# Side gate of an encoder layer: bias added by one-row products on TensorE, sigmoid read from the banks by ScalarE

## The reference

```python
    f = moe(x.reshape(B * T, D), ...).reshape(B, T, D)
    x = layer_norm(ALPHA * x + f, ln2_g, ln2_b)
    return x + jax.nn.sigmoid(x @ w_ple_gate + b_ple_gate) * (p_l @ w_ple_proj)
```

## Time and profile before

| | |
|---|---|
| median of 3 runs | 1488.61 us (1481.96 to 1497.39) |
| profiled execution | 1481.6 us, of which the span of instructions is 1479.8 us |
| PE busy | 1404.2 us, 95% of the span |
| DVE busy | 601.0 us, 41% |
| ACT busy | 275.6 us, 19% |
| gate products (L1442), both layers | 117.2 us of PE, 256 instructions |

### The profile page before, as it was taken

How to read it: one execution, slowest core, us unless ns; L and a number is a source line. 1 busy time by engine, 2 the same in 40 slices (tenths; PEclk the granted TensorE clock), 3 DMA queues, 4 the chain that set the end, 5 groups by cost and what they waited for, 6 DMA issues and landing times.

```text
span 1479.8 us, 20569 instructions
## 1 busy us (share of the span) xinstructions
PE 1404.2 (95%) x6970; PEld 727.9 (49%) x6970; DVE 601.0 (41%) x1224; ACT 275.6 (19%) x671; POOL 117.9 (8%) x137
## 2 busy tenths in 40 slices
PE   7999999898899999998999999989989999999898
PEld 3787446453344443443457874464533444433344
DVE  5086785545210110106530867855453110101356
ACT  1211335212100110011131013442121001000112
POOL 2100000110000000004000000011100000000300
PEclk9999999999999999999999999999999999999999
DMA  8714003354399999948031240033544999999821
GB/s 299 261 59 151 25 1 118 143 193 153 132 414 426 427 427 425 393 178 291 0 130 58 78 153 3 1 118 143 194 152 136 380 428 426 427 427 426 323 69 47
DMA packets 80940, 319.47 MB, mean 216 GB/s; under 512 B 12684, under 2 KB 15044, under 8 KB 56300
## 3 DMA queue, kind: packets, MB, share of 16 engines
q1 hardware_dynamic: 66772, 272.19, 47.0%
q0 software_dynamic: 9280, 29.68, 5.4%
q10 hardware_dynamic: 4824, 16.75, 2.8%
HBM read 429.21 MB, written 29.67 MB: 310 GB/s over the span
## 4 chain that ended last, share of the span: by engine, by line
PE 79%; DMA 7%; DVE 5%; issue 3%; SPq 2%; ACT 2%; DVEq 1%; POOL 0%; ACTq 0%; POOLq 0%
PE psum L1362 17%; PE psum L953 12%; PE psum L1389 9%; PE psum L1442 8%; PE psum L1021 8%; PE psum L1225 7%; PE psum L923 4%; DMA region<-in_w_exp_up_dram 3%; PE psum L892 2%; PE psum L871 1%; PE psum L1363 1%; PE psum L1276 1%; PE psum L1341 1%; PE psum L1006 1%; SPq L709 1%
## 5 line engine op out<-in xcount | busy, mean ns | idle before, releaser
L1362 PE MATMUL psum<-ring,xT 128*64 128x512 f32 x800 | 355.6, 596 | 9.1 <-DMA region<-in_w_exp_gate_dram 4.0
L1363 PE MATMUL psum<-region,xT 128*64 128x512 f32 x800 | 356.5, 597 | 0.0
L1362 PEld LDWEIGHTS psum<-ring,xT 128*64 128x64 f32 x800 | 107.2, 138 | 210.9 <-issue 210.8
L1389 PE MATMUL psum<-ring,region 128*64 128x512 f32 x400 | 176.2, 592 | 4.4 <-issue 2.8
L953 PE MATMUL psum<-xT,ring 128*128 128x272 f32 x768 | 176.5, 393 | 0.0
L1390 PE MATMUL psum<-region 128*64 128x512 f32 x400 | 176.3, 593 | 0.0
L953 PEld LDWEIGHTS psum<-xT,ring 128*128 128x128 f32 x768 | 145.8, 190 | 30.1
L2233 DVE COPY region<-psum 128x512 f32<-128x512 f32 x23 | 15.9, 691 | 319.7 <-PE psum L1390 319.7
L1021 PE MATMUL psum<-ring,xT 128*128 128x512 f32 (+1 forms) x288 | 132.5, 603 | 0.6 <-DVE region L1882 0.6
L1442 PE MATMUL psum<-ring,xT 128*128 128x512 f32 x256 | 117.2, 614 | 1.7 <-DMA ring<-in_w_ple_gate_dram 0.9
L778 POOL TENSOR_TENSOR rr<-rq,half 128x1 f32<-128x1 f32 (+4 forms) x41 | 56.9, 1387 | 716.6 <-DVE rq L1748 267.7
(11 more groups left out here) (286 smaller groups left out, 1456.9 us busy)
## 6 DMA issues: line engine op xcount, KB each, us to landing
region<-in_w_exp_gate_dram SPq DMA_DIRECT2D x54, 1024.0 KB
ring<-in_w_exp_gate_dram SPq DMA_DIRECT2D x54, 1024.0 KB
region<-in_w_exp_up_dram SPq DMA_DIRECT2D x54, 1024.0 KB
ring<-in_w_exp_up_dram SPq DMA_DIRECT2D x54, 1024.0 KB
ring<-in_w_exp_down_dram SPq DMA_DIRECT2D x54, 1024.0 KB
region<-in_w_exp_down_dram SPq DMA_DIRECT2D x54, 1024.0 KB
ring<-in_w_in_dram SPq DMA_DIRECT2D x24, 1024.0 KB, 8.4
expert_results<-region ACTq DMA_DIRECT2D x23, 512.0 KB, 7.7
```

The costliest lines, as they stand in the source:

```text
L1362: pe.matmul(bank[b][front, :], xeT[:, kc, front], ring[:, BLOCK_SLOT[u], kc % 4, :], start=kc == 0, stop=kc == KC - 1)
L1363: m = pe.matmul(bank[b][last, :], xeT[:, kc, last], back[:, UNIT_ROOM[u], kc % 4, :], start=kc == 0, stop=kc == KC - 1)
L1389: pe.matmul(bank[5 + half][front, :], hT[:, 2 * n + q, front], ring[:, BLOCK_SLOT[u], 2 * q + half, :], start=n + q == 0, stop=n + q == 2)
```

## The change

Four things are changed in the side-gate stage, in both layers.

- PE begins each half of tiles 0 to 3 with one product of a row of ones (`ones[0:1, :]`, set once at the start) by the bias row `bple[0:1, :]`, 128 x 512 out of a contraction of one row. The eight products that follow add to it. For tile 4 it is four such products of 32 x 128 a half. PE also waits, once a layer, for `hw_zero` and for `ln2p_in`.
- ACT takes the sigmoid straight out of the bank into `gt` (tile 4: in four quarters into `ye`) and frees the bank. For tiles 1 to 3 it first waits for `x_ready` of the tile before, whose `gt` DVE must have read. `gates(t - 2)` now stands ahead of the turned tile t.
- DVE loses the two sums of each tile, and the sums of tile 4.
- The semaphore `pg_sum` and the copies `sample_out("pg", n)` go.

```diff
@@ PE
                 turn_tile(l, "x2", x2_ready, 0)
+                pe.wait_ge(hw_zero, 1)
+                pe.wait_ge(ln2p_in, 48 * (l + 1))
                 for t in range(TILES):
                     turned(l, ("x2", t, 0))
                     turned(l, ("x2", t, 1))
...
                         if t == 4:
-                            m = sample_sum(pe, B(key), range(KC), ...)
+                            pe.sem_inc(pe_pass, 1)
+                            for c in range(4):
+                                pe.matmul(B(key)[DEC * c:DEC * c + DEC, 0:P], ones[0:1, 0:DEC], bple[0:1, n * 512 + c * P:n * 512 + (c + 1) * P], start=True, stop=False)
+                            m = sample_sum(pe, B(key), range(KC), ..., begun=True)
                             m.then_inc(full[use(key)], 1)
                             continue
+                        pe.matmul(B(key)[0:ROWS[t], :], ones[0:1, 0:ROWS[t]], bple[0:1, n * 512:(n + 1) * 512], start=True, stop=False)
                         for kc in range(KC):
...
-                            m = pe.matmul(B(key)[0:ROWS[t], :], xT[:, kc, span(t)], slot(u)[:, kc % 4, :], start=kc == 0, stop=kc == KC - 1)
+                            m = pe.matmul(B(key)[0:ROWS[t], :], xT[:, kc, span(t)], slot(u)[:, kc % 4, :], start=False, stop=kc == KC - 1)
@@ ACT
         def gates(sc, l, t):
+            if 0 < t < 4:
+                sc.wait_ge(x_ready, TILES * (l + 1) + t)
             for n in range(2):
-                sc.wait_ge(pg_sum, 2 * (TILES * l + t) + n + 1)
-                sc.activation(gt[0:ROWS[t], n * 512:(n + 1) * 512], gt[0:ROWS[t], n * 512:(n + 1) * 512], ACT.Sigmoid).then_inc(pg_sig, 1)
+                key = ("pg", t, n)
+                c = slice(n * 512, (n + 1) * 512)
+                sc.wait_ge(full[use(key)], taken(l, key) + 1)
+                if t == 4:
+                    m = quarters(sc, ye[0:DEC, c], B(key), ACT.Sigmoid)
+                else:
+                    m = sc.activation(gt[:, c], B(key)[:, :], ACT.Sigmoid)
+                m.then_inc(free[use(key)], 1)
+                sc.drain()
+                sc.sem_inc(pg_sig, 1)
...
                 for t in range(TILES):
+                    if t > 1:
+                        gates(sc, l, t - 2)
                     for s in range(2):
...
-                    if t > 1:
-                        gates(sc, l, t - 2)
                 gates(sc, l, TILES - 2)
                 if l + 1 < DEPTH:
                     x0_turned(l + 1, 0)
-                for n in range(2):
-                    sample_out("pg", n)
                 gates(sc, l, TILES - 1)
@@ DVE
                 def gate_add(t):
...
-                    for n in range(2):
-                        key = ("pg", t, n)
-                        c = slice(n * 512, (n + 1) * 512)
-                        if t == 4:
-                            ve.wait_ge(sample_ready, 4 * l + 2 + n + 1)
-                            ve.tensor_tensor(gt[0:r, c], ye[0:r, c], bple[0:r, c], ALU.add)
-                        else:
-                            filled(l, key)
-                            ve.tensor_tensor(gt[0:r, c], B(key)[0:r, :], bple[0:r, c], ALU.add)
-                        ve.drain()
-                        ve.sem_inc(pg_sum, 1)
-                        if t < 4:
-                            ve.sem_inc(free[use(key)], 1)
                     for n in range(2):
                         c = slice(n * 512, (n + 1) * 512)
                         ve.wait_ge(pg_sig, 2 * (TILES * l + t) + n + 1)
```

More of the change, by code:

```diff
@@ L492, in encoder_step @@
         sample_ready = sem("sample_product_ready")
-        pg_sum = sem("ple_gate_sum")
         pg_sig = sem("ple_gate_sig")
@@ L862, in rows_out, with sample_sum @@
             m.then_inc(oT_full, 1)
-        def sample_sum(pe, out, chunks, rows, weights):
+        def sample_sum(pe, out, chunks, rows, weights, begun=False):
             pe.sem_inc(pe_pass, 1)
@@ L870, in sample_sum @@
                 for c in range(4):
-                    m = pe.matmul(out[DEC * c:DEC * c + DEC, 0:P], rows(kc), weights(kc)[:, c * P:(c + 1) * P], start=kc == 0, stop=kc == KC - 1)
+                    m = pe.matmul(out[DEC * c:DEC * c + DEC, 0:P], rows(kc), weights(kc)[:, c * P:(c + 1) * P], start=kc == 0 and not begun, stop=kc == KC - 1)
             return m
@@ L1434, in _ @@
                         if t == 4:
-                            m = sample_sum(pe, B(key), range(KC), lambda kc: xT[:, kc, SEQ:TOK], lambda kc: slot(("pg", n, kc // 4))[:, kc % 4, :])
+                            pe.sem_inc(pe_pass, 1)
+                            for c in range(4):
+                                pe.matmul(B(key)[DEC * c:DEC * c + DEC, 0:P], ones[0:1, 0:DEC], bple[0:1, n * 512 + c * P:n * 512 + (c + 1) * P], start=True, stop=False)
+                            m = sample_sum(pe, B(key), range(KC), lambda kc: xT[:, kc, SEQ:TOK], lambda kc: slot(("pg", n, kc // 4))[:, kc % 4, :], begun=True)
                             m.then_inc(full[use(key)], 1)
                             continue
+                        pe.matmul(B(key)[0:ROWS[t], :], ones[0:1, 0:ROWS[t]], bple[0:1, n * 512:(n + 1) * 512], start=True, stop=False)
                         for kc in range(KC):
@@ L1463, in values, with quarters @@
             sc.activation(o_tok[:, i % 2, :], bank[6 + i % 2][:, :], ACT.Copy).then_inc(sq_done, 1)
-        def quarters(sc, dst, src):
+        def quarters(sc, dst, src, func=ACT.Copy):
             for c in range(4):
-                m = sc.activation(dst[:, c * P:(c + 1) * P], src[DEC * c:DEC * c + DEC, 0:P], ACT.Copy)
+                m = sc.activation(dst[:, c * P:(c + 1) * P], src[DEC * c:DEC * c + DEC, 0:P], func)
             return m
         def gates(sc, l, t):
+            if 0 < t < 4:
+                sc.wait_ge(x_ready, TILES * (l + 1) + t)
             for n in range(2):
-                sc.wait_ge(pg_sum, 2 * (TILES * l + t) + n + 1)
-                sc.activation(gt[0:ROWS[t], n * 512:(n + 1) * 512], gt[0:ROWS[t], n * 512:(n + 1) * 512], ACT.Sigmoid).then_inc(pg_sig, 1)
+                key = ("pg", t, n)
[8 more added lines that the diff above has]
+                sc.sem_inc(pg_sig, 1)
         @block.scalar
@@ L2049, in _ @@
                         if t == 4:
-                            ve.wait_ge(sample_ready, 4 * l + n + 1)
+                            ve.wait_ge(sample_ready, 2 * l + n + 1)
                             ve.scalar_tensor_tensor(xs, xs, ALPHA, ye[0:r, n * 512:(n + 1) * 512], ALU.mult, ALU.add)
@@ L2277, in gate_add @@
                 def gate_add(t):
-                    r = ROWS[t]
+                    r, gate = ROWS[t], ye if t == 4 else gt
                     ve.drain()
-                    for n in range(2):
-                        key = ("pg", t, n)
-                        c = slice(n * 512, (n + 1) * 512)
-                        if t == 4:
-                            ve.wait_ge(sample_ready, 4 * l + 2 + n + 1)
-                            ve.tensor_tensor(gt[0:r, c], ye[0:r, c], bple[0:r, c], ALU.add)
-                        else:
-                            filled(l, key)
-                            ve.tensor_tensor(gt[0:r, c], B(key)[0:r, :], bple[0:r, c], ALU.add)
-                        ve.drain()
-                        ve.sem_inc(pg_sum, 1)
-                        if t < 4:
-                            ve.sem_inc(free[use(key)], 1)
                     for n in range(2):
@@ L2295, in gate_add @@
                         ve.wait_ge(pg_sig, 2 * (TILES * l + t) + n + 1)
-                        ve.tensor_tensor(gt[0:r, c], gt[0:r, c], plp[0:r, PLP_AT[t], c], ALU.mult)
+                        ve.tensor_tensor(gate[0:r, c], gate[0:r, c], plp[0:r, PLP_AT[t], c], ALU.mult)
                     ve.drain()
-                    ve.tensor_tensor(x[0:r, t, :], x[0:r, t, :], gt[0:r, :], ALU.add).then_inc(x_ready, 1)
+                    ve.tensor_tensor(x[0:r, t, :], x[0:r, t, :], gate[0:r, :], ALU.add).then_inc(x_ready, 1)
                 ve.wait_ge(ln2p_in, 48 * (l + 1))
```

## The result

| | before | after |
|---|---|---|
| median | 1488.86 us (1481.96 to 1497.39, 4 runs) | 1512.19 us (1505.41 to 1513.65, 4 runs) |
| profiled execution | 1481.6 us, span 1479.8 | 1511.1 us, span 1509.2 |
| mean granted clock of it | 0.988 | 0.979 |

The ratio of after to before is 1.0152, with an interval of 1.0114 to 1.0191: the change makes the kernel some 23 us slower. The page of after shows DVE's share down and PE's busy time up; of that only a part is the new products.

The account below looks back on a forecast made before the run. PE's instructions were taken to bound the side-gate stage. Added products 20.0 us, less 0.15 hidden and 1.43 at the end, gave 18.4 us: 1507.0 us on the median of 1488.61, range 1495 to 1516.

Parts of the forecast that it names:

- PE's instructions are the path in this stage: Side-gate stage: PE sets the time; what is taken from DVE is worth nothing except in the last 4.57 us.
- The columns, 0.86 us a product: Tiles 0 to 3: each one-row product is two float32 instructions of 512 columns at 0.43 us each.
- The shape, 0.28 us: Each one-row product between full-shaped ones: going to another array shape and back costs 0.28 us, bounds 0 and 0.40.
- The sample tile, 0.9 us a layer: Tile 4: eight added instructions of 128 columns a half, 0.45 us a half with the way back.
- What hides it: 0.15 us in layer 1: Layer 1's stage start: waiting for the gate's weights covers 0.15 us of added PE work; layer 0's waits hide none.
- The end, 1.43 us less: Chain over ACT and DVE behind PE's last product: 3.14 us against 4.57.
- What is moved costs nothing: Moved gates, sigmoids and bank releases on ACT: covered by some 8 us of slack, so costed at nothing.
- that rival: PE's turn of tile 3 waits on DVE's 11.2 us stall; change frees up to 22.4 us: 1484.6 us, chance 3%.
- The clock's stretch at the stage's start: Rival: one-row product lengthens the half-rate clock stretch at both stage starts by 1.6 us each: 1510.2 us, chance 10%.
- The only-columns rival: Change of shape costs nothing for one-row products: 13.1 us slower, 1501.7 us on the median, chance 13%.

Follow-up runs that it names:

- run without products: Changed kernel with the row-of-ones products taken out and the gate's bias left out: median 1484.2 us, ratio 0.997 to the kernel before.
- 128-row run: Changed kernel with bias products contracting 128 rows of 1/128 instead of one row of ones: median 1499.6 us, ratio 1.0104 to the kernel before.

## Why the prediction was right

The time lies in the range that was given, and the sign and the bound of 1% were forecast; the sum was 18.4 us, 19.9 are measured at equal clock, 23 between the medians of the first runs. The median of after lies 5 us above the number that was given; it is in the range because the range's upper end was taken from the slowest run of before. Point by point:

- *PE's instructions are the path in this stage.* Right. Products alone cost what the whole change costs (+20.8 against 19.9 and 1.4 of gain), and the rest of the change leaves PE's timeline as it was.
- *The columns, 0.86 us a product.* Right to the hundredth: 8.60 - 7.74 between full-shaped neighbours.
- *The shape, 0.28 us.* This term was too small. It is 0.39 where both neighbours are full-shaped, so the row of the gathered sums (0.40) was the nearer one, and not that of the short contraction, which I took. By sixteen products the difference would be 1.8 us; where a neighbour has another shape already (the gathered sums and the transposes of the sample tile), one product costs 0.93 to 0.99 us, so some of it comes back. The rule of the Trainium skill (TensorEngine Tiling (Array Packing), Key Properties) that a change of tiling mode drains TensorE agrees with the trace here: the surcharge is there with one row and gone with 128.
- *The sample tile, 0.9 us a layer.* 771.80 - 767.33 = 4.47 us against 3.63 before: 0.84. Right.
- *What hides it: 0.15 us in layer 1.* Not seen: the first product starts 0.89 us behind the turned tile's transposes, like the first product before, and there it waits for the turned tile's copy and not for the weights.
- *The end, 1.43 us less.* Right in the trace, 1.41. That the time gains by it is not shown (see the run without products).
- *What is moved costs nothing.* Right: no new wait of PE in the stage. DVE had the turned tile 3 ready at 722.18 + 1.28 = 723.46 and PE asked for it at 740.65, 17 us later; before, the slack was 1.7 us. So DVE's 11 us were worth nothing, as forecast, and that rival fell.

```profile
712.74 0.69 DVE L2296 TENSOR_TENSOR region<-region 128x512 f32<-128x512 f32 x1 [3.32 <-ACTq L1488]
...
722.18 1.28 DVE L1783 SCALAR_TENSOR_TENSOR x<-x,rr,region 128x1024 f32<-128x1024 f32 x1 [0.44 <-POOL rr L777]
...
740.65 1.04 PE L891 MATMUL psum<-ident,x 128*128 128x128 f32 x8
```

- *The clock's stretch at the stage's start.* It stayed about as long: in layer 0 product and first block take 702.89 - 693.25 = 9.64 us against 8.02 for the next ones (703.86 to 711.88), 1.6 lost where 1.55 were before. In layer 1 it grew somewhat: 1435.53 - 1423.86 = 11.67 us against the same 8.02, 3.65 lost where 3.1 were before; the rival's 1.6 a layer did not come.

```profile
1423.86 2.04 PE L1442 MATMUL psum<-region,ones 1*128 1x512 f32 x2 [0.89 <-ACT xT L1499]
...
1435.53 1.04 PE L891 MATMUL psum<-ident,x 128*128 128x128 f32 x8
```

- *The only-columns rival* fell for this kernel, and is what the 128-row run measures: I had 13.1 us for it, 13.4 came.

What the prediction missed is the spread that the clock brings: the first runs of after had a mean clock of 0.9795, the runs of before 0.982, and 0.0025 by 1.19 us a thousandth is some 3 us of the 23.

## What to carry to other kernels

An engine's work is worth removing only where another engine waits for it: here 16 sums of a half-idle DVE were exchanged for 16 products on the engine that set the pace. If a bias must be added on TensorE, give the product the shape of its neighbours (replicated rows and a factor of 1/128 instead of one row of ones) and, where the bias may be rounded, a short type; that took the price from 1.25 to 0.21 us. And where TensorE waits just ahead of a long stage, a few products that nobody reads can keep its clock up, as far as they cover the wait.

## What the runs showed of the hardware

A product that contracts 128 rows was cheaper than one that contracts one row, by 0.39 us, when only the latter stood in another array shape than its neighbours. A bfloat16 product among float32 ones in the same bank paid no such surcharge (0.21 us for 512 columns, one instruction, against 0.86 in float32).

The granted clock of one and the same stretch, with the same instructions, was 1.00 in some profiled executions and 0.75 in others (246 to 280 us, above), and each 0.001 of the mean clock moved the time by 1.19 us; nearly all of the 18 us between the fastest and the slowest run of the kernel before go with it. At the stage's start a filled wait of PE gave 1.5 and 3.7 us back; with 2.04 us left unfilled, a part of the slow start returned. Whether the stretch in the mixing part could be kept on the full clock in the same way was not tried.
